# Second attention's bias rows: made at the border of the blocks, spread from ScalarE's queue

## The reference, cut to what matters

```
first_block:   h = h + hybrid_mixer(rms_norm(h));  h = h + sq_relu_mlp(rms_norm(h))
second_block:  ada = c @ w_ada + b_ada;  h = rmsnorm(x, g) * (1 + scale1) + shift1;  proj = h @ w_in
  forgetting_attention:        s = q.k * d**-0.5 + F[t] - F[s]           (F: cumulated log forget gates)
  indexer_sparse_attention:    logits = q.k * d**-0.5 + rel_bias[t5_bucket(t - s)]   on the top-128 keys
```

## Time and profile before

| | us |
|---|---|
| median of three runs | 1350.88 |
| the profiled execution: its time | 1350.03 |
| its span | 1348.2 |
| TensorE busy | 1337.3 (99%) |
| weight loads of TensorE | 1093.1 (81%) |
| VectorE busy | 762.4 (57%) |
| ScalarE busy | 526.4 (39%) |
| GpSimd busy | 564.2 (42%) |

### The profile page before, as it was taken

One profiled execution on the slowest core, in us unless ns is written; L12 is line 12 of the kernel. 1 busy time (PEld: TensorE's weight loads), 2 busy tenths in 40 slices (PEclk: granted clock), 3 DMA queues, 4 the chain that ended last, 5 costly groups with the idle time before them and its releaser, 6 DMA issues.

```text
span 1348.2 us, 18053 instructions
## 1 busy us (share of the span) xinstructions
PE 1337.3 (99%) x6378; PEld 1093.1 (81%) x6378; DVE 762.4 (57%) x1095; ACT 526.4 (39%) x831; POOL 564.2 (42%) x230
## 2 busy tenths in 40 slices
PE   9999999999999999999999999999999999999998
PEld 8888878888888888876877777888878888888886
DVE  3555678575665655878788774443463241432355
ACT  6344234423413224253466665322355133242333
POOL 5334344554653645425222224444434534345351
PEclk9999999999999999999999999999999999999999
DMA  7232345656655646423322323334422423323221
GB/s 231 79 96 80 91 137 169 181 169 174 186 173 152 198 132 173 114 78 95 63 77 65 95 66 92 109 94 111 124 78 94 125 79 110 93 81 121 78 94 63
DMA packets 212807, 155.74 MB, mean 116 GB/s; under 512 B 8932, under 2 KB 193760, under 8 KB 212744
## 3 DMA queue, kind: packets, MB, share of 16 engines
q1 hardware_dynamic: 212280, 154.43, 39.6%
q10 hardware_dynamic: 464, 0.48, 0.1%
HBM read 152.75 MB, written 4.74 MB: 117 GB/s over the span
## 4 chain that ended last, share of the span: by engine, by line
PE 53%; DVE 1%; ACT 1%; issue 0%; POOL 0%; ACTq 0%; DVEq 0%
PE ps L586 28%; PE ps L1145 11%; PE ps L1089 3%; PE ps L1026 2%; PE ps L1005 1%; PE ps L992 1%; PE ps L1175 1%; PE ps L978 1%; PE ps L979 1%; PE ps L982 0%; PE ps L965 0%; PE ps L939 0%; PE ps L940 0%; PE ps L943 0%; PE ps L1114 0%
## 5 line engine op out<-in xcount | busy, mean ns | idle before, releaser
L547 POOL TENSOR_TENSOR w_lo<-raw,w_hi 128x1024 fp32r<-128x1024 f32 x222 | 561.2, 2536 | 754.3 <-ACT w_hi L1231 734.2
L586 PE MATMUL ps<-u_hi,w_hi 128*128 128x512 f32 x944 | 376.7, 399 | 0.8 <-POOL w_lo L547 0.5
L586 PE MATMUL ps<-u_hi,w_lo 128*128 128x512 f32 x944 | 368.5, 390 | 0.0
L586 PE MATMUL ps<-u_lo,w_hi 128*128 128x512 f32 x944 | 367.9, 390 | 0.0
L1231 ACT ACTIVATE w_hi<-raw 128x1024 fp32r<-128x1024 f32 x222 | 231.8, 1054 | 290.6 <-PE ps L586 112.9
L586 PEld LDWEIGHTS ps<-u_hi,w_lo 128*128 128x128 f32 x944 | 177.2, 188 | 37.7
L586 PEld LDWEIGHTS ps<-u_hi,w_hi 128*128 128x128 f32 x944 | 178.2, 189 | 35.6 <-POOL w_lo L547 0.9
L586 PEld LDWEIGHTS ps<-u_lo,w_hi 128*128 128x128 f32 x944 | 177.6, 188 | 34.2
L586 PE MATMUL ps<-y_hi,w_hi 128*128 128x512 f32 x320 | 125.2, 391 | 0.1
L586 PE MATMUL ps<-y_hi,w_lo 128*128 128x512 f32 x320 | 124.5, 389 | 0.0
L586 PE MATMUL ps<-y_lo,w_hi 128*128 128x512 f32 x320 | 124.5, 389 | 0.0
(11 more groups left out here) (333 smaller groups left out, 1884.6 us busy)
## 6 DMA issues: line engine op xcount, KB each, us to landing
raw<-w_in SPq DMA_DIRECT2D x69, 512.0 KB, 3.8
raw<-w_mlp SPq DMA_DIRECT2D x64, 512.0 KB, 4.0
adaw<-w_ada SPq DMA_DIRECT2D x32, 768.0 KB, 4.6
raw<-w_up SPq DMA_DIRECT2D x32, 512.0 KB, 6.7
raw<-w_down SPq DMA_DIRECT2D x32, 512.0 KB, 6.0
raw<-w_out SPq DMA_DIRECT2D x16, 512.0 KB, 4.3
bias_rows<-bias_rows SPq DMA_DIRECT2D x4, 635.0 KB
xtok<-x SPq DMA_DIRECT2D x4, 512.0 KB, 6.8
```

The costliest lines, as they stand in the source:

```text
L547: pool.tensor_tensor(w_lo[:, s, :], raw[:, s, :], w_hi[:, s, :], ALU.subtract).then_inc(lo_ready[s], 1)
L586: last = pe.matmul(ps[0:cols, bank, :], w[:, s, c], r[:, k, :], start=(k == ks[0] and w is w_hi and r is r_hi), stop=(k == ks[-1] and w is ...
```

## The change

Four things move. The two bias matmuls go from `st_ret`'s projections to the border of the blocks, between the two halves of `roots_turned`, and the vectors are turned in a function of their own; ScalarE's two copies to `fbrow` go behind the norm's outputs m = 4 and m = 6. Half of the `ada_rows` matmuls takes the place of the two fillers in `both_sums`. The copy to HBM and the four spreads go from SyncE's queue to ScalarE's: the copy behind the cast of `st_val`'s slot 0, the spreads behind the casts of slots 2 and 3 of turn 0, of slot 3 of turn 1 and behind `value_evac(st_val, 2)`. SyncE loads `oneh` and `rbias` later, in `st_out`, into memory that block 1's retention no longer needs. Its wait for all spreads stands now ahead of `tab_load(4)`, and no longer ahead of `tab_load(0)`; a wait of VectorE for the copy falls away. Not in the diff below are the lines that free the old buffers' places.

```diff
--- before.py
+++ after.py
...
@@ -283,6 +278,10 @@
         mix.close()
         adaw = sb("adaw", [P, 2, 6 * D // 4], where=one)
         gones, pick = sb("gones", [P, 2], where=one), sb("pick", [P, 64], where=one)
+        fbrow = sb("fbrow", [HEADS, NREL], where=one)
+        sb("squares_kept", [P, 3 * T + P], where=one)
+        oneh = sb("oneh", [BUCKETS, NREL], where=one)
+        rbias = sb("rbias", [BUCKETS, HEADS], where=one)
         one.close()
 
         two = ExitStack()
@@ -362,23 +361,6 @@
                 for s, at in enumerate([W1_RQ, W1_RK, W1_RG]):
                     load(st_ret, s, j, (whole, cols(w_in, at + j * P)))
 
-            def brow_copy():
-
-                sp.wait_ge(sem("brow_read"), 2)
-                sp.dma_start(bias_rows[:, 0:1, :],
-                             bass.AP(fbrow[:].tensor, fbrow[:].offset, [fbrow[:].ap[0], [0, 1], [1, NREL]])
-                             ).then_inc(sem("brow_out"), 16)
-
-            def brow_spread(j):
-
-
-                if j == 0:
-                    sp.wait_ge(sem("brow_out"), 16)
-                h = 2 * j * P * NREL
-                sp.dma_start(bass.AP(bias_rows.tensor, h + NREL, [[P * NREL, 2], [NREL, P - 1], [1, NREL]]),
-                             bass.AP(bias_rows.tensor, h, [[P * NREL, 2], [0, P - 1], [1, NREL]])
-                             ).then_inc(sem("brow_out"), 16)
-
             def value_rows(s, k0, k1, done):
 
                 sp.dma_start(raw[:, s, k0 * QW:k1 * QW].rearrange("p (k m) -> p k m", m=QW),
@@ -401,18 +383,14 @@
                     src = src.rearrange("(j p) -> j p", p=P)
                 sp.dma_start(vrow[VAT[name]:VAT[name] + n, :], src
                               ).then_inc(sem("vrow_in"), 16)
-            sp.dma_start(oneh[:], tab[0:BUCKETS, TAT["onehot"]:TAT["onehot"] + NREL]).then_inc(sem("bias_in"), 16)
-            sp.dma_start(rbias[:], rel_bias_2).then_inc(sem("bias_in"), 16)
             sp.dma_start(bfor[:], b_forget_2.rearrange("(h a) -> h a", a=1)).then_inc(sem("rope_in"), 16)
             sp.dma_start(rope[:], tab[:, TAT["cos"]:TAT["cos"] + 2 * T].rearrange("p (a t) -> p a t", a=2)
                           ).then_inc(sem("rope_in"), 16)
             ret_loads(0)
             sp.dma_start(fades[:], tab[:, TAT["keep"]:TAT["keep"] + P + 4 * NQ]).then_inc(sem("decay_in"), 16)
             ret_loads(1)
-            brow_copy()
             with sp.Fori(2, NQ) as j:
                 ret_loads(j)
-            brow_spread(0)
             with sp.Fori(0, NQ) as j:
                 for s, at in enumerate([W1_CC, W1_CH, W1_CB]):
                     load(st_conv, s, j, (whole, cols(w_in, at + j * P)))
@@ -423,14 +401,15 @@
                     ds(q, 1), d, :, ds(i * 3 * D + b * 3 * D // 2, 3 * D // 2)]
                 sp.dma_start(adaw[:, b, :], src.rearrange("q p n -> p (q n)")).then_inc(sem(f"ada_in{b}"), 16)
 
-            brow_spread(1)
             for i in range(KC // 4):
                 for s in range(4):
                     load(st_out, s, i, (whole, cols(w_out, i * 4 * P + s * P)))
                     if i == 1 and s == 2:
                         sp.wait_ge(sem("mix_done"), 1)
                         ada_load(0, 0, 0, 0)
-            brow_spread(2)
+                        sp.dma_start(oneh[:], tab[0:BUCKETS, TAT["onehot"]:TAT["onehot"] + NREL]
+                                     ).then_inc(sem("bias_in"), 16)
+                        sp.dma_start(rbias[:], rel_bias_2).then_inc(sem("bias_in"), 16)
 
             def quarter(q, last=False):
 
@@ -452,9 +431,7 @@
                         if s == 2 and not (last and i == 1):
                             ada_load(q + i, 1 - i, 1 - i, 0)
 
-            quarter(0)
-            brow_spread(3)
-            with sp.Fori(1, NF - 1) as q:
+            with sp.Fori(0, NF - 1) as q:
                 quarter(q)
             quarter(NF - 1, True)
 
@@ -478,6 +455,8 @@
             def tab_load(p):
                 if p >= 2:
                     sp.wait_ge(sem("att_logit"), 8 * (p - 1))
+                if p == NQ:
+                    sp.wait_ge(sem("brow_out"), 16 * (NQ + 1))
                 dst = tab2[:, 2 * (p % 2):2 * (p % 2) + 2, :]
                 if p < NQ:
                     src = bass.AP(forget_rows.tensor, 2 * p * T, [[0, P], [T, 2], [1, T]])
@@ -490,7 +469,6 @@
             value_loads(1, W2_DV)
             att_loads(0)
             sp.wait_ge(sem("ada_sum"), 4)
-            sp.wait_ge(sem("brow_out"), 16 * (NQ + 1))
             sp.wait_ge(sem("forget_out"), 16)
             tab_load(0)
             tab_load(1)
...
@@ -609,8 +587,7 @@
                     t = slice(i * P, (i + 1) * P)
                     pe.matmul(ps[:, TR, 2 * i:2 * i + 1], nt[:, 1, t], ones[:, 0:1], start=(i == 0), stop=False)
                     pe.matmul(ps[:, TR, 2 * i + 1:2 * i + 2], nt[:, 2, t], ones[:, 0:1], start=False, stop=False)
-                for _ in range(2):
-                    pe.matmul(ps[:, SB, 0:2 * P], ones[:], small[:, 0:2 * P], start=True, stop=True)
+                between()
                 pe.wait_ge(sem("norm_sq"), sums_before("n3") + KC)
                 pe.wait_ge(sem("squares"), 4)
                 for i in range(NT):
@@ -663,12 +640,15 @@
             def bias_rows_made():
 
                 pe.wait_ge(sem("bias_in"), 32)
-                pe.matmul(ps[0:HEADS, SB, :], rbias[:], oneh[:, 0:T], start=True, stop=True)
-                pe.matmul(ps[0:HEADS, OU, 0:P], rbias[:], oneh[:, T:NREL], start=True, stop=True
+                pe.wait_ge(bank_free[2], st_idx.turn(2, 0))
+                pe.matmul(ps[0:HEADS, 2, :], rbias[:], oneh[:, 0:T], start=True, stop=True)
+                pe.matmul(ps[0:HEADS, TR, 2 * P:3 * P], rbias[:], oneh[:, T:NREL], start=True, stop=True
                           ).then_inc(sem("brow_done"), 1)
 
+            def vectors_turned():
+
                 pe.wait_ge(sem("vrow_in"), 16 * (len(VECS) - 1))
-                pe.transpose(ps[:, OU, P:P + NVEC], vrow[:], ident[0:NVEC, 0:NVEC]).then_inc(sem("brow_done"), 1)
+                pe.transpose(ps[:, OU, 0:NVEC], vrow[:], ident[0:NVEC, 0:NVEC]).then_inc(sem("vec_turned"), 1)
 
 
             def ret_scores(p):
@@ -776,10 +756,9 @@
                 last = pe.transpose(ps[:, SA, i * P:(i + 1) * P], osb[:, i * P:(i + 1) * P], ident)
             last.then_inc(sem("gain_turned"), 1)
             unit(st_ret, 0, 0, u_hi, u_lo, part=(2, KC), opens=False)
-            bias_rows_made()
+            vectors_turned()
             unit(st_ret, 1, 0, u_hi, u_lo)
             unit(st_ret, 2, 0, u_hi, u_lo)
-            pe.wait_ge(sem("brow_read"), 2)
             pe.wait_ge(sem("vec_ready"), 1)
             ret_scores(0)
             with pe.Fori(1, NQ) as j:
@@ -889,10 +868,10 @@
                     ada_turned(0)
 
             pe.wait_ge(sem("acc_done"), PIECES + 1)
-            both_sums()
-            ada_rows(1, 0, closes=False)
+            both_sums(lambda: ada_rows(1, 0, closes=False))
             ada_rows(2, 1, opens=False)
             roots_turned(0)
+            bias_rows_made()
             roots_turned(1)
 
             def idx_units():
@@ -1032,6 +1011,8 @@
                         for i in range(NT):
                             if s == 0 and kk == 0:
                                 pe.wait_ge(bank_free[i], st_idx.turn(2, 0) if r == 0 and i == 2 else st_val.turn(i, r))
+                                if r == 0 and i == 2:
+                                    pe.wait_ge(sem("brow_read"), 1)
                             last = block(kk, i)
                         if kk == 1:
                             last.then_inc(used[s], 1)
@@ -1289,6 +1270,13 @@
                                    bias=ada[:, shift + m:shift + m + 1]).then_inc(sem("norm_hi"), 1)
                     if m == 2:
                         ada_row_copy(1)
+                    if m == 4:
+                        act.wait_ge(sem("brow_done"), 1)
+                        act.activation(fbrow[:, 0:T], ps[0:HEADS, 2, :], ACT.Copy, scale=HD ** 0.5
+                                       ).then_inc(sem("brow_read"), 1)
+                    if m == 6:
+                        act.activation(fbrow[:, T:NREL], ps[0:HEADS, TR, 2 * P:3 * P], ACT.Copy, scale=HD ** 0.5
+                                       ).then_inc(sem("brow_read"), 1)
 
             for s in range(1, SLOTS):
                 act.sem_inc(hi_ready[s], 1)
@@ -1344,11 +1332,8 @@
             value_evac(st_rv, 0, 2, NT)
             act.wait_ge(sem("gain_turned"), 2)
             act.activation(r1[:], ps[:, SA, :], ACT.Copy).then_inc(sem("r1_ready"), 1)
-            act.wait_ge(sem("brow_done"), 1)
-            act.activation(fbrow[:, 0:T], ps[0:HEADS, SB, :], ACT.Copy, scale=HD ** 0.5).then_inc(sem("brow_read"), 1)
-            act.wait_ge(sem("brow_done"), 2)
-            act.activation(fbrow[:, T:NREL], ps[0:HEADS, OU, 0:P], ACT.Copy, scale=HD ** 0.5).then_inc(sem("brow_read"), 1)
```

(27 more changed lines are left out.)

5 lines of the change are left out of this document (removed).

## The result

The changed kernel took 1367.65 us (median of five, 1365.47 to 1370.68) beside 1350.91 us of the kernel before on the same chip: a ratio of 1.0125, 95% interval 1.0114 to 1.0136. That is 16.7 us slower, where 9.9 were forecast, and just above the upper end of the range, 1367.5. The profiled execution is the slowest of the five, 1370.68 us, span 1368.9.

A forecast was written before the change was run, and what follows sets the result against it. TensorE, busy 1337.3 of 1348.2 us, was taken to bound the kernel. The terms -1.17 - 0.1 + 9.7 + 1.5 = +9.9 us took 1350.88 to 1360.8 us, range 1349.0 to 1367.5.

The forecast's parts named there:

- Projections of block 1: Block 1: without the bias matmuls the turn of the vectors starts at 37.45 instead of 38.62, saving 1.17 us.
- Border: Border of the blocks: half of ada_rows replaces the fillers, bias matmuls nearly fit; -0.1 us, bounds -0.4 and +0.4.
- `forget_rows` behind the spreads: ScalarE's queue, block 2: forget_rows waits behind two spreads, so SyncE goes on at 646.7 instead of 632.37.
- ScalarE's issue: ScalarE's queue: DMA issues, even one blocked behind a full queue, were put at no cost to the time.
- The load's landing: Second head pair's first load: lands at 669.9, TensorE resumes at 673.5 instead of 663.75, +9.7 us, bounds 0 and +17.4.
- The half: Load behind the gate's write: half of the earlier 6.2 us lateness, 3.1 us, added because part passes while pieces queue.
- Turns of pieces: Spread's two engines: two queues share an engine piece by piece in turn; tables, gate and load take 18.1 us.
- The clock: TensorE after its wait of some 10 us: the granted clock falls, +1.5 us, bounds 0 and 3.9.
- The short transfer: Rival, ScalarE's queue: forget_rows shares no engine with the spreads, SyncE goes on at 632.4; 1349.6 us, chance 0.11.
- the loads did not win the engines: Rival, loads after 646.7: held up, but they get through within 13 us, landing by 660; 1349.6 us, chance 0.16.
- The third: Rival: SyncE's transfers wait for all the spreads, TensorE resumes at 681; 1368.9 us, chance 0.09.
- Eight engines: Block 2 transfers: by the skill's rule forget_rows (8 rows) uses eight engines, the spread's two among them.

The follow-up runs named there:

- e1: Changed kernel with the four spreads put behind the transfer of forget_rows in ScalarE's queue: 1356.58 us.
- e4: Changed kernel with the write of gate_vec behind the two loads of the second head pair in SyncE's queue: 1362.84 us.
- e6: Changed kernel with the write of gate_vec ahead of SyncE's wait for forget_rows: 1362.10 us.
- e9: Changed kernel with the write of gate_vec far later, behind the loads of the fifth pair: 1355.61 us.
- e2: Changed kernel with the two fillers back in both_sums and both halves of ada_rows behind the sums: 1367.53 us.
- e5: Kernel before with only the fillers out and half of ada_rows in their place: 1351.30 us, ratio 1.0002.
- e8: Changed kernel with one spread of all 8 heads at the place of spread 0, the other three gone: 1348.96 us, ratio 0.9984.
- e3: Changed kernel with the edits of both e1 and e2, spreads behind forget_rows and fillers back: 1355.00 us.
- e7: Changed kernel with fillers back and one spread of all 8 heads, issued behind the cast of st_val's slot 1: 1350.49 us, ratio 0.9995.

## Why the prediction was wrong, step by step

- **Projections of block 1, -1.17.** Right. The turn of the vectors follows the projection directly; at 187 us the profiled executions of the changed kernel and of e1 to e4 and e6 to e9 are 0.5 to 1.2 us ahead of the kernel before. The rest is the start: in the changed kernel's profile the first projection begins 0.8 us later than in that of before.
- **Border, -0.1.** Within its bounds for the executions in which the clock stays (+0.1 us in e1, e2 and e4), wrong for the changed kernel's profiled one, +3.9 us. I took the fillers for time that anything could fill. The new sequence, one and two columns, then `ada_rows` on 32 columns, keeps TensorE busy to 100% and yet the clock falls to 0.5 in three of the seven profiled executions without fillers and with no added matmuls (the changed kernel, e5, e8; not in e1, e4, e6, e9), and in none of the four with fillers (the kernel before, e2, e3, e7). That the fillers hold the clock is not shown by so few. The mean granted clock of all executions does not bear it out: it is 0.999 or more in 9 of 11 runs of e8 (without fillers) and 8 of 12 of e7 (with), in 3 of 11 of e5 (without) and 8 of 15 of the kernel before beside it (with).
- **`forget_rows` behind the spreads.** Right, and to about 1 us: SyncE goes on at 650.28, 3.4 us of which are the border, where 646.7 was forecast; in e4 and e9, without the fall at the border, at 645.7 and 645.9. e1 shows it by the order alone. ScalarE's issue that was held for 5.76 us cost nothing, as was said.
- **The load's landing: the step that failed is the size of one term.** Forecast were 23.2 us from SyncE's going on, measured 29.1. By the runs: tables and load taking turns with the spreads 16.0 (13.7 forecast), the gate's pieces 5.5 (6.4), and the slow memory behind the gate's write 7.6, where I took 3.1, half of the 6.2 us by which the load was late before. The half was a guess that it would pass while pieces queue. It does not: in that stretch little moves on any queue, the spread's rows neither (20 rows in 656 to 664 us, against 132 in the same 8 us of e9), so the whole of it is added. The runs show it added wherever the write stands before the load's end: behind the load's issue in e4 (7.6), ahead of `forget_rows` in e6, where SyncE goes on 7.1 us later than in e9. TensorE's wait came out at 16.3 us where 8 to 12 were forecast. With 7.6 for 3.1 the sum would have been 14.4 us, 1365.3; with 16.0 for 13.7 and 5.5 for 6.4 as well, 15.8 us, 1366.7. What is left to 1367.65 is less than the runs differ among themselves.
- **Turns of pieces.** Chosen without a row, so by luck, and borne out. In 674 to 676 us of the kernel after there are 65 packets, 33 rows of the spread on ScalarE's queue and 32 pieces of the load on SyncE's:

```profile
q10 hardware_dynamic: 33, 0.08, 10.5%
q1 hardware_dynamic: 32, 0.02, 2.7%
```

  The Trainium skill ("DMA: Bandwidth & Descriptors", section "Queues, rings and completion order") has an engine take a whole packet of pieces, 9 to 17 as a rule, before it turns to the next queue. The trace does not agree: in each of seven stretches of 0.12 us, from 674.12 to 674.96, the two engines together have two rows and two pieces, so each takes one row and one piece in turn; nine rows in a run would hold an engine for 0.88 us.
- **The clock, +1.5.** The wait did bring the clock down, and the size is right, 1.5 us in the changed kernel, but in part by luck: the same matmuls lost 2.8 us in e2 behind a wait of 16.7 us, and 2.6 in e9 behind one of 3.1. So the loss does not follow the length of the wait, for which I took the low side.
- **The rivals.** The short transfer did not slip past, and the loads did not win the engines. The third, with everything behind all spreads, forecast 1368.9, nearest to the time but not for its reason: the load landed at 679.37, before the last spread ended.
- **Eight engines.** That `forget_rows` shares the spread's engines was argued from the Trainium skill (the same page, section "Why a DMA increments its semaphore by 16 and not by 1"). The same rule gives a spread of eight heads eight engines; e8 agrees, with 1,016 rows in about 16 us instead of 50 and a share of 0.51 of the 16 engines.

What stays open: why the clock falls in some executions and not in others, and what divides the runs of e7 (and those of the kernel before, at 1350.7 and at 1351.8). The mean granted clock says that lost clock goes with it: of the kernel before it is 0.999 or 1.000 in the faster group, 0.997 to 0.999 in the slower. Where it is lost no trace shows, since the profiled executions of these two kernels are of the faster group.

## What to carry to other kernels

Before a transfer is moved to another queue, list what stands behind it there and who waits for that: the four spreads were harmless in a queue that ran ahead and cost, together with the write of `gate_vec`, some 16 us in front of one 16 KB transfer that another queue waited for. Such a spread, with a slowest dimension of 2, holds two engines for 12.5 us, and a load beside it gets one of its pieces through for each row there; give such a copy a slowest dimension with more to divide (e8). Ask of a write of many single elements what stands behind it: here the slow stretch was added whole to the next load. And before taking a filler matmul out, look at the granted clock of the stretch in several executions, not at the busy share; whether the fillers here hold the clock the runs do not show.

## What the runs showed of the hardware that was not expected

- A write of 1,024 single 4-byte pieces to memory is followed by about 8 us in which all DMA engines together move 8 to 36 GB/s (18 in 640 to 646 us of the kernel before, 36 in 656 to 664 after, 8 in 660 to 668 of e4, 14 in 632 to 640 of e6); moved away, the stretch runs at the usual rate of a lone spread, 50 GB/s (e9). In e9 nothing was under way behind the write, so its effect there can't be seen.
- TensorE's clock was granted at 0.50 for 10 us while the engine was busy to 100%, with the sums of 1 and 2 columns and the `ada_rows` on 32 columns before and in it. Behind a wait of 16.3 us, in which it fell, it came back about 3 us after work had begun again.
- On a queue with two spreads under way ScalarE's next DMA issue took 5.76 us instead of 0.31; nothing on the path waited for ScalarE then. In e6 it took 12.40 us.
